# Two hybrid decoder layers on one core: gate tiles in pieces between the transposes of the front, compression moved ahead, sigmoid and copies one split sooner

## The reference

```python
def hybrid_layer(x, ...):
    c_q, c_kv, k_r, n_q, n_kv, n_gate, m_gate = jnp.split(x @ w_in, offsets, axis=-1)
    q = (rms_norm(c_q, mla_q_norm) @ mla_w_uq).reshape(B, S, MLA_HEADS, 64 + 32)
    q_nope = q[..., :64]; q_rope = apply_rope(q[..., 64:], *rope_mla)
    kv = (rms_norm(c_kv, mla_kv_norm) @ mla_w_ukv).reshape(B, S, MLA_HEADS, 64 + 64)
    k_nope, v = kv[..., :64], kv[..., 64:]
    k_rope = apply_rope(k_r[:, :, None, :], *rope_mla)[:, :, 0, :]
    y_mla = mla_attention(q_nope, q_rope, k_nope, k_rope, v) @ w_branch_mla
    ...                                  # n_q, n_kv: rotated queries, keys, values of the sparse branch
    kc = compress_blocks(k_cmp, ck_pe, ck_w1, ck_w2)        # gelu((blocks + pe) @ w1) @ w2
    vc = compress_blocks(kvs[:, :, 1], cv_pe, cv_w1, cv_w2)
    nsa_gates = jax.nn.sigmoid(n_gate.reshape(B, S, NSA_HEADS, 3))
    y_nsa = nsa_attention(qn, kc, vc, k_sel, v_sel, k_win, v_win, nsa_gates) @ w_branch_nsa
    g_mla, g_nsa = jnp.split(jax.nn.sigmoid(m_gate), 2, axis=-1)
    mixed = (g_mla * y_mla + g_nsa * y_nsa) @ w_out
    x = layer_norm(ALPHA * x + mixed, ln1_g, ln1_b)
    return layer_norm(ALPHA * x + peer(x, ...), ln2_g, ln2_b)
```

## Time and profile before

| | |
|---|---|
| time, median of 3 runs | 2095.61 us (2093.98 to 2096.58) |
| the profiled execution, its own time | 2093.44 us |
| its span, first to last instruction | 2091.7 us |
| TensorE busy | 2032.6 us, 97% of the span |
| VectorE, ScalarE, GpSimd busy | 1492.7 (71%), 1177.3 (56%), 688.2 us (33%) |
| the chain that ended last | TensorE 87%, VectorE 5%, DMA 4%, ScalarE 2% |
| mean granted TensorE clock | 0.996 of full speed |
| loads: weight tile, w1 part, blank table write | 512, 256 and 1024 KB each |

### The profile page before, as it was taken

The page is one execution under the profiler, slowest core; times in us unless marked ns, Lnnn a source line. Parts: engine busy times, 40 slices in busy tenths (PEclk is TensorE's granted clock), DMA queues, the critical chain, the costliest instruction groups (busy, mean ns, idle before and its releaser), DMA issues.

```text
span 2091.7 us, 36550 instructions
## 1 busy us (share of the span) xinstructions
PE 2032.6 (97%) x11636; PEld 1745.5 (83%) x11636; DVE 1492.7 (71%) x2958; ACT 1177.3 (56%) x2023; POOL 688.2 (33%) x646
## 2 busy tenths in 40 slices
PE   8999999999999999999999999999999999999997
PEld 6987888888887888888788878988888878888886
DVE  6657668888898655555576567688888985555556
ACT  4446456776558644544444454576765685444443
POOL 1100003777874311111120000058778561111111
PEclk9999999999999999999999999999999999999999
DMA  5654545777773466666555634567766615666674
GB/s 192 202 174 139 179 145 190 190 186 188 190 187 100 135 216 229 210 224 226 180 194 180 221 118 152 174 185 189 191 187 186 190 56 191 215 224 215 230 221 144
DMA packets 176197, 384.12 MB, mean 184 GB/s; under 512 B 48944, under 2 KB 81744, under 8 KB 176112
## 3 DMA queue, kind: packets, MB, share of 16 engines
q1 hardware_dynamic: 139632, 372.26, 53.2%
q0 software_dynamic: 36480, 10.81, 5.5%
HBM read 365.04 MB, written 17.96 MB: 183 GB/s over the span
## 4 chain that ended last, share of the span: by engine, by line
PE 87%; DVE 5%; DMA 4%; ACT 2%; issue 1%; POOL 0%; SPq 0%; POOLq 0%; DVEq 0%; ACTq 0%
PE wide L1687 35%; PE acc L1673 11%; PE wide L1673 11%; PE acc L1676 6%; PE wide L1676 5%; PE acc L1662 3%; PE acc L1663 3%; PE acc L1664 3%; PE acc L2168 3%; DMA raw<-in_front 2%; DMA gt<-table 1%; PE tr L1865 1%; ACT hi L681 1%; DVE lo L1037 1%; PE wide L2128 1%
## 5 line engine op out<-in xcount | busy, mean ns | idle before, releaser
L681 ACT ACTIVATE hi<-raw 128x1024 fp32r<-128x1024 f32 (+1 forms) x644 | 676.6, 1051 | 713.2 <-DMA raw<-in_peer_v 338.1
L1027 DVE TENSOR_TENSOR lo<-raw,hi 128x1024 fp32r<-128x1024 f32 x520 | 635.3, 1222 | 374.2 <-ACT hi L681 372.4
L624 POOL DMA_INDIRECT table<-picks,spots x256 | 454.5, 1775 | 282.2 <-DVE spots L1497 156.6
L1687 PE MATMUL wide<-hi,w_lo 128*128 128x512 f32 x1016 | 314.3, 390 | 6.8 <-DVE w_lo L1602 6.5
L1687 PE MATMUL wide<-hi,w_hi 128*128 128x512 f32 x1016 | 312.9, 389 | 0.0
L1687 PE MATMUL wide<-lo,w_hi 128*128 128x512 f32 x1016 | 312.9, 389 | 0.0
L657 POOL TENSOR_TENSOR big<-big,gt 128x128 f32 x248 | 117.7, 475 | 571.7 <-DMA gt<-table 559.9
L1673 PE MATMUL acc<-xT,hi 128*128 128x512 f32 x1024 | 256.8, 393 | 0.0
L1673 PE MATMUL wide<-xT,hi 128*128 128x512 f32 x992 | 248.4, 392 | 0.0
L1687 PEld LDWEIGHTS wide<-hi,w_lo 128*128 128x128 f32 x1016 | 189.7, 188 | 50.2 <-DVE w_lo L1602 5.2
L1687 PEld LDWEIGHTS wide<-hi,w_hi 128*128 128x128 f32 x1016 | 190.7, 188 | 39.7
(11 more groups left out here) (326 smaller groups left out, 2879.5 us busy)
## 6 DMA issues: line engine op xcount, KB each, us to landing
raw<-in_peer_u SPq DMA_DIRECT2D x256, 512.0 KB, 3.5
raw<-in_peer_v SPq DMA_DIRECT2D x254, 512.0 KB, 4.1
raw<-in_front SPq DMA_DIRECT2D x114, 512.0 KB, 3.8
table<-blank SPq DMA_DIRECT2D x16, 1024.0 KB, 7.4
gt<-table SPq DMA_DIRECT2D x254, 64.0 KB, 3.8
ln_par<-in_ln POOLq DMA_DIRECT2D x10, 512.0 KB, 5.3
raw<-in_front SPq DMA_DIRECT2D x12, 384.0 KB, 3.2
w<-in_cmp_w POOLq DMA_DIRECT2D x16, 256.0 KB, 4.1
```

The costliest lines, as they stand in the source:

```text
L624: pool.indirect_dma_start(table[l], bass.IndirectOffsetOnAxis(spots[:, u, k:k + 1], 0), picks[:, 2, 0, u * TOPK + k:u * TOPK + k + 1], Non ...
L681: nc.scalar.activation(hi[:, s, :width], raw[:, s, :width], ACT.Identity).then_inc(hi_done, 1)
L1027: nc.vector.tensor_tensor(lo[:, s], raw[:, s], hi[:, s].bitcast(F32), ALU.subtract).then_inc(lo_done, 1)
L1687: ins = mm(wide[:, tt, 512 * h:512 * h + width], a[:, tok], w[:, off:off + width], start=first and k == 0, stop=last and k == 2)
```

## The change

TensorE: each half of a B tile's tokens is finished before the other begins, and the second bank of `acc` is waited for only before the second half. Gate tiles 4, 5 and 6 are computed in pieces of whole 128-row blocks (`gate_part`) which stand between other work; the query transposes move from before gate tile 4 to around the compressed scores, the key transposes from after the compression products into gate tile 6. A wait for the last copies out of `tr` is added before the attention scores. ScalarE: the sigmoid of the sparse gates comes one split sooner, and the copies of queries and keys follow the new order of transposes. VectorE: the copies out of `acc` come one split sooner and both halves together, `blk` and one split come before the query rotation, and the copies of the keys come after the compressed scores. GpSimd: the last two parts of w1 are loaded when tiles 27 and 28 are done (before: 24 and 26), the product keys after the last key transposes.

The diff, without its unchanged lines:

```diff
--- before.py
+++ after.py
@@ -116 +116 @@
-X_XT, X_CD, X_NQ, X_KT, X_Q, X_K, X_HT, X_PC, X_AT, X_XT2, X_PK = 0, 4, 6, 8, 10, 14, 18, 20, 24, 42, 44
+X_XT, X_CD, X_NQ, X_KT, X_HT, X_Q, X_K, X_PC, X_AT, X_XT2, X_PK = 0, 4, 6, 8, 10, 12, 16, 20, 24, 42, 44
@@ -607 +607 @@
-                for q, n in ((6, T_B), (7, T_B + 2)):
+                for q, n in ((6, T_B + 3), (7, T_UKV)):
@@ -611 +611 @@
-                pool.wait_ge(tr_ready, l * NTR + X_HT)
+                pool.wait_ge(tr_ready, l * NTR + X_PC)
@@ -761 +761 @@
-                for n in range(T_B, T_UKV):
+                for n in range(T_B, T_UKV - 1):
@@ -768 +768 @@
-                for n in range(T_UKV, T_MG):
+                for n in range(T_UKV - 1, T_MG):
@@ -784,3 +783,0 @@
-                for g in range(4):
-                    tt, hg = divmod(g, 2)
-                    heads_copy(X_Q + g, qT[:QKD, 4 * hg:4 * hg + 4, tt * P:(tt + 1) * P], QKD, hg)
@@ -794,2 +790,0 @@
-                for tt in range(TT):
-                    heads_copy(X_K + 2 * tt, kT[:QKD, 0:4, tt * P:(tt + 1) * P], QKD, 0)
@@ -797,0 +793,3 @@
+                for g in range(4):
+                    tt, hg = divmod(g, 2)
+                    heads_copy(X_Q + g, qT[:QKD, 4 * hg:4 * hg + 4, tt * P:(tt + 1) * P], QKD, hg)
@@ -801,0 +800 @@
+                heads_copy(X_K, kT[:QKD, 0:4, 0:P], QKD, 0)
@@ -802,0 +802 @@
+                heads_copy(X_K + 2, kT[:QKD, 0:4, P:2 * P], QKD, 0)
@@ -1241 +1241,2 @@
-                    tile_step(l, T_UKV + tt)
+                for n in range(T_UKV - 1, T_MG):
+                    tile_step(l, n)
@@ -1253,6 +1253,0 @@
-                for tt in range(TT):
-                    dve.wait_ge(wide_read[tt], OPEN + l * NWIDE + W_UQ + 1)
-                    part = q_tok[:, tt, :, NOPE:]
-                    st.link(rotate(part, part, cos_m[:, tt], sin_m[:, tt], HEADS, ROPE, rope_a, rope_b))
-                    dve.sem_inc(q_ready, 1)
-
@@ -1271,0 +1267,7 @@
+                tile_step(l, T_MG + 1)
+                for tt in range(TT):
+                    dve.wait_ge(wide_read[tt], OPEN + l * NWIDE + W_UQ + 1)
+                    part = q_tok[:, tt, :, NOPE:]
+                    st.link(rotate(part, part, cos_m[:, tt], sin_m[:, tt], HEADS, ROPE, rope_a, rope_b))
+                    dve.sem_inc(q_ready, 1)
+
@@ -1277 +1278,0 @@
-                tile_step(l, T_MG + 1)
@@ -1279,2 +1279,0 @@
-                for tt in range(TT):
-                    tr_copy(l, X_K + 2 * tt + 1, kT[:QKD, 4:8, tt * P:(tt + 1) * P], tr[:QKD, 1].rearrange("p (h t) -> p h t", h=4))
@@ -1305,0 +1305,2 @@
+                for tt in range(TT):
+                    tr_copy(l, X_K + 2 * tt + 1, kT[:QKD, 4:8, tt * P:(tt + 1) * P], tr[:QKD, 1].rearrange("p (h t) -> p h t", h=4))
@@ -1668,0 +1670,11 @@
+            def columns_part(s, xh, xl, bank, blocks):
+
+                for k in blocks:
+                    c = slice(k * P, (k + 1) * P)
+                    dst = acc[:, bank, :SEQ]
+                    mm(dst, lo[:, s, c], xh[:, k], start=k == 0, stop=False)
+                    mm(dst, hi[:, s, c], xl[:, k], start=False, stop=False)
+                    ins = mm(dst, hi[:, s, c], xh[:, k], start=False, stop=k == DK - 1)
+                if DK - 1 in blocks:
+                    ins.then_inc(slot_free[s], 1)
+
@@ -1833,0 +1846,8 @@
+                def gate_part(c, blocks):
+
+                    n = MG_TILE[c]
+                    if 0 in blocks:
+                        acc_free(l, MG_USE[c])
+                        tile_ready(l, n // SLOTS, n % SLOTS)
+                    columns_part(n % SLOTS, xT_hi, xT_lo, MG_USE[c] % 2, blocks)
+
@@ -1836,2 +1856 @@
-                for b in range(2):
-                    acc_free(l, A_B + b)
+                acc_free(l, A_B)
@@ -1842,4 +1861,6 @@
-                    for kk in range(2):
-                        k = 2 * q + kk
-                        c = slice(kk * WB, (kk + 1) * WB)
-                        for tt in range(TT):
+                    for tt in range(TT):
+                        if q == 0 and tt == 1:
+                            acc_free(l, A_B + 1)
+                        for kk in range(2):
+                            k = 2 * q + kk
+                            c = slice(kk * WB, (kk + 1) * WB)
@@ -1873,0 +1895 @@
+                gate_part(4, range(0, 2))
@@ -1876,0 +1899,2 @@
+                    if tt == 0:
+                        gate_part(4, range(2, 4))
@@ -1879,4 +1903,3 @@
-                def transpose_qk(first, src):
-                    for g in range(4):
-                        tt, hg = divmod(g, 2)
-                        transpose_heads(first + g, [src[:, tt, 4 * hg + j] for j in range(4)], QKD)
+                def transpose_qk(first, src, tt):
+                    for hg in range(2):
+                        transpose_heads(first + 2 * tt + hg, [src[:, tt, 4 * hg + j] for j in range(4)], QKD)
@@ -1884,3 +1907 @@
-                pe_.wait_ge(q_ready, l * TT + TT)
-                transpose_qk(X_Q, q_tok)
-                gate_tile(4)
+                gate_part(4, range(4, DK))
@@ -1903,2 +1924 @@
-                pe_.wait_ge(k_ready, l * TT + TT)
-                transpose_qk(X_K, k_tok)
+                gate_part(5, range(0, 3))
@@ -1907 +1926,0 @@
-                gate_tile(5)
@@ -1909,0 +1929 @@
+                gate_part(5, range(3, 6))
@@ -1920,0 +1941,3 @@
+                gate_part(5, range(6, DK))
+                pe_.wait_ge(q_ready, l * TT + TT)
+                transpose_qk(X_Q, q_tok, 0)
@@ -1934 +1957,6 @@
-                gate_tile(6)
+                transpose_qk(X_Q, q_tok, 1)
+                gate_part(6, range(0, 4))
+                pe_.wait_ge(k_ready, l * TT + TT)
+                transpose_qk(X_K, k_tok, 0)
+                gate_part(6, range(4, DK))
+                transpose_qk(X_K, k_tok, 1)
@@ -1935,0 +1964,2 @@
+                for b in range(2):
+                    pe_.wait_ge(tr_read[b], OPEN + l * (NTR // 2) + X_PC // 2)
```

## The result

| | before | after |
|---|---|---|
| median of the runs that were compared | 2094.8 us (2089.41 to 2096.58, 4 runs) | 2074.72 us (2073.79 to 2076.44, 4 runs) |
| the profiled execution, its own time | 2093.44 us | 2074.37 us |
| its span | 2091.7 us | 2072.6 us |
| mean granted TensorE clock | 0.996 | 0.999 |

The ratio is 0.9911 (95% interval 0.9899 to 0.9923): faster by 0.9%. The forecast was 2079 us, in a range of 2073 to 2087.

What follows compares the result with a forecast made beforehand. TensorE's chain of waits was taken as the bound. Savings 14.2 - 0.2 + 0.4 - 1.8 + 4.3 = 16.9 us took 2093.4 to 2076.5; 2.2 for earlier runs' median made 2078.7, say 2079, range 2073 to 2087.

Steps and rivals of the forecast that it cites:

- the kr wait: Gate tile 2 waiting after the w_ukv tiles: 2.5 us plus 0.3 for both layers, 2.6 counted as gone.
- 0.9 for the compression: New TensorE wait per layer for VectorE's blk before the compression; bounds 0.4 and 1.5, so 1.8 us given back.
- Ten kinds: TensorE waits standing once per layer on lines the change touches: 11.0 us for both layers, 14.2 with refills.
- the lower bound: Compression's wait for blk if only cmpT copies and blk's 4.28 us set it: at least 0.4 us per layer.
- the upper one: Compression's wait for blk if VectorE's splits of tiles 32 and 33 come up to 1.6 us later: 1.5 us.
- pipeline refill: Each of 20 TensorE waits costs about 0.16 us more than its idle time: 3.2 us.
- the forecast's loads of w1: Parts 6 and 7 load one and two tiles later, shortening the w_ukv wait: 0.4 us taken, bounds nothing and 2.4.
- the 4.3 us: Clock loss at the compressed scores and gate tiles 6 and 7, both layers, all counted as gone.
- The first rival: The clock falls all the same around the compressed scores: 2083 us in both layers, 2081 in one; chance 0.25.
- the fourth: Split gate tiles no longer hold the clock, from first gate piece to gate tile 7: slower, 2102 us; chance 0.05.
- Rival 3: Time is given back in attention, where tile loads share DMA engines with blank writes: 2087 us; chance 0.07.
- Rival 2: VectorE becomes the bound before the compression, 1.5 us of wait per layer instead of 0.9: 2082 to 2085; chance 0.14.

Runs made afterwards that it cites:

- second profile of the changed kernel: The changed kernel, unaltered, run again beside the version with three further edits: 2075.7 us (5 runs), ratio 0.9918 to the kernel before.
- first occasion: The changed kernel's first measurement against the kernel before: 2074.72 us against 2094.8 us, 4 runs each, ratio 0.9911.
- the narrow fillers: Changed kernel with gate tile 5 ahead of the small products, and eight 128-column products replacing the query transposes on each side of the compressed scores: 2087.06 us.
- the kernel before with fillers: Kernel before, nothing moved, plus three 512-column filler products behind the small products and three behind the compressed scores, per layer: 2091.82 us, ratio 1.0001.

## Why the prediction was right

*The sum.* 16.9 us were forecast. The fronts gave 17.3 in the first pair of profiles and 18.2 with the second profile of the changed kernel, and the runs side by side with 15 of before gave 2092.73 - 2075.7 = 17.0; the medians of the first occasion differ by 20.1. The size was right, and so was the mechanism of idle time filled with work, but for the kr wait and half of the clock below. That it met 17.0 to a tenth is in part luck: 0.4 for w_ukv and 0.9 for the compression were chosen within bounds of 0 to 2.4 and 0.4 to 1.5.

*The step that was off* is the last: 2.2 us were added because the three runs shown lay above the profiled execution. Later runs of before have medians of 2091.8 to 2092.7, under its 2093.4. By its own time, 2076.5, the forecast would have been 0.8 us from the second occasion's median and 1.8 from the first's.

*Waits.* Ten kinds, 11.0 us, all gone; with 0.2 staying, 0.4 saved at w_ukv and 1.8 given back at the compression, 9.4 us less idle was forecast and 9.5 is what the lists show, 0.4 of it from the hidden layer's transposes, which the forecast left out. (Its L1916 is a small product, not the second compression product; and its own 0.3 us left per layer at gate tile 2 would be 0.6, where the sum takes 0.2. Nothing stayed there.) The w_ukv wait fell by 0.4 in sum, as taken. The compression's wait was 0.6 and 1.6 (0.6 and 0.6 the second time) for 0.9 each. In layer 0 the lower bound, the chain of copies and blocks, decides; in layer 1 the upper one, VectorE's queue behind late tiles, does in the first profile: 1.6 for 1.5. That each pipeline refill costs 0.16 beyond its wait is borne out by the sum alone; no run measures it.

*The kr wait: right sum, wrong cause.* The forecast gave it to the sigmoid's place. With the sigmoid put back it was gone all the same, since tile 30 lands sooner: its load went out at 91.97 us (91.87 before) and its split began 4.7 us later (6.4 before), so it was carried faster and not issued sooner. The later loads of w1 are the likeliest reason: with the sigmoid put back they went out at 93.82 and 97.85 us, before at 88.57 and 91.99, the last just behind tile 30's load. So the forecast's loads of w1 (they moved by three and two tiles, not by one and two), taken at 0.4, may hold most of these 2.6 us. Loads of w1 put back alone were not run, so this is argued and not shown. The kernel may have two remedies for one wait here.

ScalarE's table load agrees with the forecast's reading: the sigmoid starts at 97.10, 0.02 us after the load's end at 95.80 + 1.28. By an estimate from the 1.38 us of drain behind a load (the Trainium skill, "ScalarE: Activation LUTs", "What ACT_TABLE_LOAD costs") it would have been 98.5. Neither trace shows a drain there.

*The pieces of gate tile 4* took two waits away and uncovered the compression's, as the forecast's 1.8 us said; uncut, the time is the same.

*The clock.* Neither profile of the changed kernel shows a fall in the fronts, so the 4.3 us went there; a mean of 0.998, which some of its runs have, can hold one fall of 3.4 us. The reason given, that the idle parts go, is half of it: the clock was also lost without idle time (the narrow fillers) and kept with 512-column products or transposes in the same places. The first rival (0.25) and the fourth (0.05) rested on transposes not holding the clock. The Trainium skill, "TensorE: Matmul & The Clock Gate", "Part 4: PE-mode transpose", says that a transpose does not count as busy in the way a product does. Here the clock stayed at 1.00 with eight transposes on either side of the compressed scores, and in the kernel before through 107.58 to 114.54 us, forty transposes and nothing else; in the profile with eight plain products of that width it fell. The measurements decide against the rule in this kernel.

*Elsewhere.* From layer 0's first score to layer 1's first B matmul the profile shows 1122.0 - 143.67 = 978.3 us before and 1109.7 - 134.60 = 975.1 after, which no step of the forecast has. Of the other profiles, those of kernels with the same work there show 974.8 to 978.7 where the clock did not fall on the way, and up to 985.0 where it did; so that difference is within the scatter between executions. Rival 3, which would have cost time there, did not happen. Rival 2 shows in layer 1 alone, as the compression's wait of up to 1.6 us.

## What to carry to other kernels

List the waits of the bounding engine that stand once per layer, and put real work of that engine into each: the sum of their idle times, 0.16 us for each pipeline refill, the new wait that the next chain brings and the clock came to within a microsecond of the side-by-side result. Follow the chain behind the last wait that you remove (copies, then blocks here), for it sets what is left; reordering its engine's queue does nothing in a layer where that engine waits for the chain anyway. Look at how much the runs behind a profile differ before reading a cause from it. Judge TensorE's clock by the granted clock around narrow products and not by its busy time, and try what stands on both sides of them.

## What was not expected of the hardware

- TensorE can be busy 4.00 of 4.00 us and be granted 0.50 in the next 4 us: in the profile 32 products of 15 columns with eight of 128 columns on either side lost the clock (in two of seven runs the mean clock shows no fall), while eight transposes or three products of 512 columns of the same drawn length (1.0 to 1.1 us) kept it.
- The same three products of 512 columns did not keep it in the one profile of the kernel before with fillers (0.64 from 136 to 140 us).
- A distance of 975 us in untouched work varies by up to 4 us from one execution to another with the clock at 1.00 (974.8 to 978.7), as much as a single edit of this change is worth.
